# Lag blocks through device memory on POOL's queue, and a new order of convolution, norms, output halves and scan steps

## The chip, the cores and the metric

The program runs on 1 core of one Trainium2 chip. A core has TensorE (PE, matmuls), VectorE (DVE), ScalarE (ACT), GpSimd (POOL) and SyncE (SP), and 16 DMA engines that they share. The metric is the device time of one execution, in microseconds, as the median of several runs.

## The reference

One step of a hybrid backbone with one layer, on 128 context tokens and 512 latent tokens of width 1024. Both groups go through the same layer with their own modulation:

```python
def layer(x, cond, h0_f, h0_b, rows, p):
    sh1, sc1, g1, sh2, sc2, g2 = modulation(cond, p["w_mod"], p["b_mod"])
    h = rmsnorm(x, p["norm1_g"]) * (1 + sc1) + sh1
    y, h_f, h_b = token_mixer(h, h0_f, h0_b, rows, p)
    x = x + g1 * y
    h = rmsnorm(x, p["norm2_g"]) * (1 + sc2) + sh2
    x = x + g2 * peer(h, p["w_query"], p["sub_keys"], p["expert_u"], p["expert_v"])

def token_mixer(h, h0_f, h0_b, rows, p):
    u, cb, cc, ch = split(h @ p["w_in"])                  # 4 x 512
    y_ssm, h_f, h_b = ssm_mixer(u, h0_f, h0_b, p)         # 32 groups, 64 complex states, both directions,
                                                          # gelu, then a GLU with w_glu
    y_conv = cb * short_conv(cc * ch, p["conv_w"], p["conv_b"], rows)   # width 3
    y_ssm = rmsnorm(y_ssm, g[:D_SSM])
    y_conv = rmsnorm(y_conv per head of 64, g[D_SSM:])
    return concat(y_ssm, y_conv) @ p["w_out"], h_f, h_b
```

`peer` takes, for each token and each of 8 heads, the best 16 of 128 x 128 experts by product keys, and gathers two rows of 1024 floats for each: 640 tokens x 8 heads x 16 choices, 8 KB each. All is fp32.

## The kernel before, in words

Each engine has one program, written out by hand; semaphores join them. The scan over tokens is cut into chunks of 8 tokens: 16 of the context and 64 of the latents. The stage that the change touches runs from about 100 to 215 us, behind the modulation's first two thirds and the projection u, and ahead of the experts.

- *Modulation.* `w_mod` comes in 24 slabs of 1 MB (SP's `load_mod`, PE's `mod_slab`, 1 us each). From slab 8 on two buffers alternate, so slab n is loaded when slab n-2 is done.
- *Chunk sums.* For 16 groups g PE forms what each chunk adds to the states (`BPT` with `U`, into banks 4 and 5 in turn, `s_mm`). ACT copies each to the state array `HH`/`HHs` (`s_ev`), groups 8 to 15 of the backward direction in reversed order.
- *Lag blocks.* Within a chunk y is a sum over lags. PE forms the kernel of 15 lags (L645, `k_mm`), DVE puts it together in `Ksb` with the d_skip term (`lag_blocks`, `k_ev`), and PE selects from it by 128 small matmuls (L662) the Toeplitz blocks `M`, 128 x 128 for each of 32 groups, through banks that ACT copies out (L1217, `m_ev`).
- *Scan.* On DVE: 16 steps over the context's chunks (`scan_ctx`, then ACT's reversed copy `Hbc`), then 15 steps on the four latent segments at once, then the corrections of segments 2, 3 and 4 (`segment_products`, `segment_add`, `segment_store`), then `scan_lat`, whereupon ACT copies `Hb`.
- *Context.* PE: y (L697 to L702, needs `M`, `HH`, `Hbc`), `conv_ctx(0..2)` with 12 weight tiles of 512 KB that SP loads (`load_conv_ctx`; tile q is issued when tile q-4 is done), the turns of y, the GLU, `mod_turn(2)`, norms (`token_sums`, `spread_root`, `head_sums`, `spread_heads`), the output projection `out_ctx` (L788) with `w_o` (`woA`, `woB`), the second norm, the first query.
- *Latent y.* `y_lat(n, i)`, eight groups of 20 matmuls (L766 to L771), needs `M`, `HH` and `Hb`. Behind them PE selects the first experts (L864), DVE writes `gidx`, and POOL starts its gathers (L1935) with a ring of 8 and later 11 row buffers.
- *Experts.* 40 pairs of block and head, 16 gathers of 1 MB each; DVE forms the dot products (L1747), PE adds the weighted rows (L878). The latent half of the mixer is spread over the first 8 of them.

SP works its list in order. In before it issues `load_mod(18..23)`, waits for tile 2, then the two tiles of `w_glu`, tiles 6 and 7, `wqa`, tiles 8 and 9, and after slab 23 `woA` and tiles 10 and 11.

## Time and profile before

| | us |
|---|---|
| median of 3 runs | 1924.85 (1923.44 to 1925.14) |
| profiled execution, time | 1922.27 |
| its span, first to last instruction | 1920.1 |
| busy: PE, PE weight load | 1194.3, 475.8 |
| busy: DVE, ACT, POOL | 1382.6, 373.5, 725.1 |
| gathers L1935 | 640 |

The profile is one execution. A busy share is a mean over stages with different limits; here the first 215 us and the experts behind them differ. "L788" is line 788 of the kernel; an idle time is put down to what ended it. The clock is TensorE's granted one, as a share of full speed.

### The profile page before, as it was taken

The numbers are of one execution on the slowest core, as the hardware profiler recorded it, in microseconds if no ns is written. First come the engines' busy times: TensorE is split into PE (matmuls) and PEld (weight loads), VectorE is DVE, ScalarE is ACT, GpSimd is POOL, SyncE is SP. The second block draws the span as 40 slices with busy tenths as digits, with TensorE's granted clock in tenths as the row PEclk, the third lists the DMA queues.
The fourth block names the chain that finished last, engine by engine and source line by source line (L and its number), as shares of the span: only waits on it lengthen the run. The fifth ranks groups of instructions, "written<-read, shape, count | busy, mean of one in ns | idle before, by whom it ended". The sixth has DMA issues, their size and how long they took to land.

```text
span 1920.1 us, 21154 instructions
## 1 busy us (share of the span) xinstructions
PE 1194.3 (62%) x7716; PEld 475.8 (25%) x7716; DVE 1382.6 (72%) x3664; ACT 373.5 (19%) x845; POOL 725.1 (38%) x666
## 2 busy tenths in 40 slices
PE   6989898999777777775543343544343454444434
PEld 3569644444322322221110000111000011111001
DVE  8968567777766766669777776677777678766664
...
GB/s 372 328 209 199 257 395 414 378 416 420 390 421 399 419 422 421 420 389 422 420 422 423 421 421 421 421 421 421 422 422 421 421 421 418 422 420 421 418 420 182
DMA packets 120968, 753.16 MB, mean 392 GB/s; under 512 B 12240, under 2 KB 27856, under 8 KB 33568
## 3 DMA queue, kind: packets, MB, share of 16 engines
...
q1 hardware_dynamic: 28704, 80.69, 11.0%
...
## 4 chain that ended last, share of the span: by engine, by line
DMA 43%; PE 28%; DVE 23%; issue 2%; POOL 1%; ACT 1%; SPq 0%; DVEq 0%; POOLq 0%; ACTq 0%
DMA r<-table,gidx 31%; DVE r L1747 9%; DMA mix_r<-table,gidx 8%; PE bank L878 7%; PE bank L846 6%; PE bank L983 3%; DMA r<-w_mod 3%; DVE mix_r L1747 2%; PE bank L996 2%; PE bank L813 1%; POOL r L1935 1%; PE bank L962 1%; PE bank L855 1%; DVE i L1680 1%; PE bank L788 1%
## 5 line engine op out<-in xcount | busy, mean ns | idle before, releaser
L1935 POOL DMA_INDIRECT r<-table,gidx x542 | 607.7, 1121 | 865.3 <-PE bank L878 723.9
L1747 DVE CUSTOM_DVE_ANT_0 r<-r 128x1024 f32<-128x1024 f32 x542 | 658.1, 1220 | 246.5 <-DMA r<-table,gidx 246.0
L878 PE MATMUL bank<-r,cond 128*32 128x512 f32 x1432 | 327.2, 911 | 370.4 <-DVE cond L1759 295.2
L878 PE MATMUL bank<-r,wgt 128*32 128x512 f32 x736 | 166.8, 921 | 194.1 <-DVE wgt L1759 145.8
L1289 ACT ACTIVATE r<-r 128x2 f32<-128x2 f32 x320 | 65.1, 204 | 1013.1 <-DVE r L1747 1012.5
L878 PEld LDWEIGHTS bank<-r,cond 128*32 128x32 f32 x1432 | 37.1, 129 | 572.0 <-DVE cond L1759 437.2
L1935 POOL DMA_INDIRECT mix_r<-table,gidx x98 | 109.4, 1116 | 136.1 <-PE bank L878 117.0
L1747 DVE CUSTOM_DVE_ANT_0 mix_r<-mix_r,r 128x1024 f32<-128x1024 f32 x98 | 119.3, 1221 | 48.4 <-DMA mix_r<-table,gidx 48.2
L878 PE MATMUL bank<-mix_r,cond 128*32 128x512 f32 x264 | 91.1, 994 | 80.7 <-DVE cond L1759 63.4
L846 PE MATMUL bank<-hT_r,r 128*128 128x512 f32 x256 | 121.5, 630 | 0.9 <-ACT hT_r L1143 0.9
L878 PEld LDWEIGHTS bank<-r,wgt 128*32 128x32 f32 x736 | 18.9, 130 | 295.3 <-DVE wgt L1759 214.3
L1757 DVE SCALAR_TENSOR_TENSOR cond<-fold,r 128x32 f32<-128x32 f32 x168 | 34.8, 248 | 71.5 <-ACT r L1289 71.5
L846 PEld LDWEIGHTS bank<-hT_r,r 128*128 128x128 f32 x256 | 50.6, 203 | 75.8 <-issue 75.8
L1289 ACT ACT_TABLE_LOAD x51 | 65.4, 1283 | 0.9
L878 PE MATMUL bank<-mix_r,wgt 128*32 128x512 f32 x128 | 40.2, 930 | 38.2 <-DVE wgt L1759 35.6
L996 PE MATMUL bank<-mix_r,r 128*128 128x512 f32 x128 | 60.0, 611 | 0.0
L983 PE MATMUL bank<-hT_r,r 128*128 128x512 f32 x128 | 59.1, 604 | 0.0
L864 PEld LDWEIGHTS bank<-r,ident 128*32 128x32 f32 x1280 | 44.4, 140 | 43.6 <-DVE r L1719 36.8
L1747 DVE DVE_READ_ACCUMULATOR2_ANT r<- 128x1 f32 x640 | 52.6, 82 | 0.0
L1285 ACT ACT_TABLE_LOAD x40 | 51.3, 1283 | 0.7
L903 PE MATMUL bank<-mix_r,modrow 128*128 128x512 f32 x80 | 46.1, 712 | 3.2 <-ACT r L1304 1.9
L1757 DVE SCALAR_TENSOR_TENSOR wgt<-fold,r 128x32 f32<-128x32 f32 x88 | 18.3, 249 | 41.3 <-ACT r L1289 41.3
...
## 6 DMA issues: line engine op xcount, KB each, us to landing
r<-w_mod SPq DMA_DIRECT2D x24, 1024.0 KB, 9.7
r<-wq_heads SPq DMA_DIRECT2D x14, 1024.0 KB, 8.8
...
wq_heads<-w_query SPq DMA_DIRECT2D x8, 1024.0 KB, 12.1
r<-w_tiles SPq DMA_DIRECT2D x12, 512.0 KB, 7.8
x_r<-w_tiles SPq DMA_DIRECT2D x10, 512.0 KB, 6.0
...
r<-w_u SPq DMA_DIRECT2D x1, 2048.0 KB, 29.5
```

Of the source, the lines that this page charges most:

```text
L788: last = mm(bank[3 + m // 4][:, (m % 4) * P:(m % 4 + 1) * P], w[:, k, :], mixc[:, k, :], start=first and m in (0, 6) and k == ks[0], stop= ...
L846: last = mm(bank[2 + h][:, :], wqb[:, k, h * P:(h + 1) * P], hT[:, k, CTX:T], start=(k == 0), stop=(k == KD - 1))
L864: last = mm(bank[3][TG * s:TG * s + TG, 8 * tg:8 * tg + 8], ident[:, TG * tg:TG * tg + TG], gi[:, :, 4 * s:4 * s + 4], start=True, stop=True)
L878: last = mm(bank[ACC[b % 2][h]][to:to + TG, :], pair_weights(NPR * G + g)[:, e, :], rows[SLOT[G * TOPK + k]][:, D + h * 512:D + (h + 1) * ...
L903: last = mm(bank[at[h]][:, :], modrow[:, tg // 2, tg % 2 * P:(tg % 2 + 1) * P], h2tok[:, 512 * h:512 * h + 512], start=True, stop=True)
L983: last = mm(bank[(4, 5, 7)[r]][:, :], wtl[(tile + 2) % 3][:, k, :], hT[:, k, CTX:T], start=(k == 0), stop=(k == KD - 1))
L996: last = mm(bank[OUT_BANK[m % 3]][:, :], woA[:, m % 4, k, :], mixl[:, k, :], start=(k == 0), stop=(k == KD - 1))
L1285: A(e16, top, ACT.Exp, bias=small[:, 0:1], accum_out=small[:, 1:2]).then_inc(exp_done, 1)
L1289: A(gel[:, par, 2 * g:2 * g + 2], hid[:, par, 2 * g:2 * g + 2], ACT.Gelu_apprx_tanh).then_inc(gelu_done, 1)
L1747: V.tensor_tensor_reduce(row, row, h2r[tg], 1.0, 0.0, ALU.mult, ALU.add, hid[:, par, k:k + 1]).then_inc(dot_done, 1)
L1757: last = stt(pair_weights(n)[:, e, :], fold[:, :], gel[:, par, k:k + 1], gate[:, par, k:k + 1].broadcast_to([P, TG]), ALU.mult, ALU.mult)
L1935: G_.indirect_dma_start(rows[SLOT[j]], None, table, bass.IndirectOffsetOnAxis(gidx[:, e, k:k + 1], 0)).then_inc(row_in[SLOT[j]], 16)
```

## The change

- *Lag blocks.* PE's selecting matmuls and ACT's copies of them go. PE forms the lag kernel ahead of the chunk sums, DVE puts it together at once. POOL stores `Ksb` to `kfull` in device memory, waits for that and for chunk sums 0 to 7 (whose operand lies where `M` goes), and reads `M` back by eight loads, each for one position in the chunk, 16 partitions.
- *Chunk sums.* Groups 9, 11, 13 and 15 are copied by DVE (`s_back`).
- *PE's order.* Chunk sums, slabs 18 and 19, `conv_ctx(0)` and `(1)`, slabs 20 and 21, y, slabs 22 and 23, the turns, `conv_ctx(2)`, the GLU, `mod_turn(2)`, `head_sums`, `spread_heads`, then the convolution's half of the output projection, with the y norm within it, then the other half. All of latent y stands behind the first scores.
- *SP's order.* Each buffer's tile comes when its predecessor is done, in the new order; `wqa` behind slab 23, `woA` and tiles 10 and 11 still behind the wait for slab 23.
- *DVE.* A step's two cross products become one with its operand reversed, in `segment_products` too. The long steps are cut up (`advance_rest`), with the convolution, the norms and the halves of `mixc` between them. The residual lies ahead of segment 3, the second norm between segments 3 and 4.
- *ACT.* The order of its operations follows; `Hb` is copied behind the first scores.

The diff, cut to its core (the full order is in the list above):

```diff
                 load_conv_ctx(q)
-            for n in range(18, 24):
-                load_mod(n)
-            sp.wait_ge(zc_mm, 2)
+            load_mod(18)
+            load_mod(19)
+            for q in range(6, 8):
+                load_conv_ctx(q)
             for j in range(2):
                 sp.dma_start(wt[:, j, :, :], w_tiles[NCONV + j]).then_inc(wtg_in, 16)
-            for q in range(6, 8):
-                load_conv_ctx(q)
-            sp.wait_ge(m_mm, 2)
-            sp.dma_start(wqa, w_query[:, :, 0:DQ]).then_inc(ld_first, 16)
+            load_mod(20)
+            load_mod(21)
             for q in range(8, 10):
                 load_conv_ctx(q)
+            load_mod(22)
+            load_mod(23)
+            sp.wait_ge(lag_dma, 16)
+            sp.dma_start(wqa, w_query[:, :, 0:DQ]).then_inc(ld_first, 16)
             sp.wait_ge(mod_mm, 24)
             sp.dma_start(woA, w_o[:, 0:4, :, :]).then_inc(ld_wo, 16)
             for q in range(10, 12):
...
-                if g >= 2:
-                    pe.wait_ge(s_ev, g - 1)
+            def chunk_sums(g):
+                if g >= 10 and g % 2:
+                    pe.wait_ge(s_back, (g - 9) // 2)
+                elif g >= 2:
+                    pe.wait_ge(s_ev, min(g - 1, 4 + g // 2))
                 for j in range(2):
...
                             last = mm(bank[4 + g % 2][64 * a:64 * a + 64, (2 * j + r) * NCH:(2 * j + r + 1) * NCH],
                                       BPT[:, q, r, 64 * a:64 * a + 64], U[:, 2 * (q % NPAIR) + a, :], start=True, stop=True)
                 last.then_inc(s_mm, 1)
-                if g == 7:
-                    mod_slab(17)
             pe.wait_ge(bd_ready, 1)
...
             mod_slab(18)
             mod_slab(19)
-            pe.wait_ge(k_ev, 1)
-            pe.wait_ge(s_ev, 16)
-            for a in range(2):
...
-                        row = slice(TG * j, TG * j + TG)
-                        col32 = slice(s // 2 * TG, s // 2 * TG + TG)
-                        last = mm(bank[MBANK[a][j]][col32, :], esel[row, a, s % 2, :], Ksb[row, :, lag0:lag0 + P],
-                                  start=(s % 2 == 0), stop=(s % 2 == 1))
-                last.then_inc(m_mm, 1)
-                mod_slab(20 + a)
-            mod_slab(22)
             def conv_ctx(r):
-                pe.wait_ge(m_ev, (1, 2, 5)[r])
                 for i in range(4):
                     q = 4 * r + i
                     pe.wait_ge(wtc_in[WTC[q]], WTC[:q + 1].count(WTC[q]) * 16)
                     for k in range(KD):
                         last = mm(bank[r][:, i * P:(i + 1) * P], wtc[WTC[q]][:, k, :], hT[:, k, 0:CTX], start=(k == 0), stop=(k == KD - 1))
                     last.then_inc(zc_mm, 1)
-                    if r == 2 and i == 0:
-                        pe.wait_ge(chx_ev, 1)
...
-                        spread_root(0)
-            pe.wait_ge(m_ev, 8)
+            conv_ctx(0)
+            conv_ctx(1)
+            mod_slab(20)
+            mod_slab(21)
+            pe.wait_ge(lag_dma, 16 * (Q + 1))
+            pe.wait_ge(s_ev, 12)
+            pe.wait_ge(s_back, 4)
+            pe.wait_ge(k_ev, 1)
             pe.wait_ge(hbc_ready, 1)
             for i in range(4):
                 for term in range(5):
...
-            conv_ctx(0)
+            mod_slab(22)
...
-                pe.wait_ge(inv_ready, 2)
+                pe.wait_ge(inv_ready, 1)
                 for m in range(KS):
                     for h in range(2):
...
                 last.then_inc(inv_mm, 1)
-            mod_slab(23)
-            conv_ctx(1)
+            conv_ctx(2)
             pe.wait_ge(wtg_in, 32)
             pe.wait_ge(gtc_ev, 2)
...
-            conv_ctx(2)
+            head_sums()
+            spread_heads()
...
                 for m in (0, 1, 2, 3, 6, 7, 4, 5) if first else range(KD):
-                    if first and m == 2:
-                        head_sums()
                     if first and m == 6:
-                        spread_heads()
+                        pe.wait_ge(sqc_ready, 2)
+                        token_sums(256, sqx[0], True, True)
+                    if first and m == 4:
+                        spread_root(0)
                     if m == 4:
                         pe.wait_ge(ld_wob, 16)
...
             pe.wait_ge(ld_wo, 32)
-            out_ctx(True, range(KS), 1)
-            out_ctx(False, range(KS, KD), 2)
+            out_ctx(True, range(KS, KD), 1)
+            out_ctx(False, range(KS), 2)
             pe.wait_ge(sqc_ready, 3)
             token_sums(257, sqx[0], True, False)
-            pe.wait_ge(hb_ready, 1)
-            pe.wait_ge(mod_free, 6)
-            y_lat(0, 0)
             pe.wait_ge(sqc_ready, 4)
             token_sums(257, sqx[1], False, True)
-            y_lat(0, 1, range(1))
             spread_root(1)
-            y_lat(0, 1, range(1, 5))
             def query(u, halves=range(2)):
...
-            for i in range(4):
-                y_lat(1, i)
+            pe.wait_ge(hb_ready, 1)
+            pe.wait_ge(mod_free, 6)
+            for n in range(2):
+                for i in range(4):
+                    y_lat(n, i)
             spread_experts(0)
             turn_rows(0)
...
-            for g in range(16):
+            for g in (*range(8), *range(8, 16, 2)):
...
+            act.wait_ge(zc_mm, 4)
+            A(ccx.rearrange("p k t -> p (k t)"), bank[0][:, :], ACT.Copy).then_inc(ccx_ev, 1)
             act.wait_ge(scan_ctx, 1)
             A(Hbc[:, 0:NCC, :, :], HH[:, NCC - 1::-1, :, 1, :], ACT.Copy).then_inc(hbc_ready, 1)
             for a in range(2):
                 act.wait_ge(yc_mm, a + 1)
                 A(Yc.rearrange("p t (i a c) -> p t i a c", i=4, a=2)[:, :, :, a, :],
                   bank[4 + a][:, :].rearrange("p (i t c) -> p t i c", i=4, t=Q), ACT.Gelu_apprx_tanh).then_inc(yc_gelu, 1)
-            act.wait_ge(zc_mm, 4)
-            A(ccx.rearrange("p k t -> p (k t)"), bank[0][:, :], ACT.Copy).then_inc(ccx_ev, 1)
...
+            A(sqx[1], mixc[:, KS:KD, :].rearrange("p k t -> p (k t)"), ACT.Square).then_inc(sqc_ready, 1)
+            act.wait_ge(sqc_used, 1)
+            A(rt8, bank[1][:, 264:272], ACT.Sqrt, scale=1.0 / (DC // 8), bias=eps_c[:, 0:1]).then_inc(rms_c, 1)
             act.wait_ge(zgc_mm, 1)
             for m in range(KS):
                 A(mixc[:, m, :], bank[5][:, m * P:(m + 1) * P], ACT.Sigmoid, bias=col(COL_BGLU + m)).then_inc(sgc_ev, 1)
             mod_take(2)
             act.wait_ge(gluc_ev, 1)
             A(sqx[0], mixc[:, 0:KS, :].rearrange("p k t -> p (k t)"), ACT.Square).then_inc(sqc_ready, 1)
-            act.wait_ge(sqc_used, 1)
+            act.wait_ge(sqc_used, 2)
             A(rt1[0], bank[1][:, 256:257], ACT.Sqrt, scale=1.0 / DS, bias=eps_c[:, 0:1]).then_inc(rms_c, 1)
-            act.wait_ge(cvx_ev, 1)
-            A(sqx[1], mixc[:, KS:KD, :].rearrange("p k t -> p (k t)"), ACT.Square).then_inc(sqc_ready, 1)
...
+            act.wait_ge(scan_lat, 1)
+            A(Hb, HH[:, NCH - 1:NCC - 1:-1, :, 1, :], ACT.Copy).then_inc(hb_ready, 1)
             exps(0)
             for n in range(2):
...
-                link(tt(ta, prev, re, ALU.mult),
-                     tt(tb[:, :, 0, :], prev[:, :, 1, :], im[:, :, 0, :], ALU.mult),
-                     tt(tb[:, :, 1, :], prev[:, :, 0, :], im[:, :, 1, :], ALU.mult))
+                link(tt(ta, prev, re, ALU.mult), tt(tb, prev[:, :, ::-1, :], im, ALU.mult))
                 link(tt(ta, ta, cur, ALU.add))
                 return tt(cur, ta, tb, ALU.add)
...
+            for g in range(9, 16, 2):
+                pr = g % 8 * 2
+                dve.wait_ge(s_mm, g + 1)
+                for r in range(2):
+                    src = bank[4 + g % 2][:, 0:4 * NCH].rearrange("p (q r c) -> p c r q", q=2, r=2)[:, :, r, :]
+                    V.tensor_copy(HH[:, NCC:0:-1, r, 1, pr:pr + 2], src[:, 0:NCC, :])
+                    last = V.tensor_copy(HH[:, NCH - 1:NCC:-1, r, 1, pr:pr + 2], src[:, NCC + 1:NCH, :])
+                last.then_inc(s_back, 1)
+            dve.wait_ge(s_back, 4)
+            dve.wait_ge(s_ev, 12)
             link(V.tensor_copy(fin[:, :, :], HHs[:, NCC, :, :]))
             link(V.tensor_copy(HHs[:, NCC, :, :], ssmv[:, 3:5, :]), V.memset(HHs[:, 0, :, :], 0.0))
             for i in range(1, NCC):
                 link(advance(HHs[:, i - 1:i, :, :], HHs[:, i:i + 1, :, :], step_a, step_b, spread(AR, 1), spread(AI, 1)))
-                if i == 3:
-                    lag_blocks()
             advance(HHs[:, NCC - 1:NCC, :, :], fin[:, :, :].rearrange("p (a r) x -> p a r x", a=1), step_a, step_b,
                     spread(AR, 1), spread(AI, 1)).then_inc(scan_ctx, 1)
             rest = slice(1, NJ)
-            for i in range(1, SEG):
-                link(advance(seg[:, rest, i - 1, :, :], seg[:, rest, i, :, :], many_a, many_b, spread(AR, NJ - 1), spread(AI, NJ - 1)))
...
+            def advance_rest(lo, hi):
+                for i in range(lo, hi):
+                    link(advance(seg[:, rest, i - 1, :, :], seg[:, rest, i, :, :], many_a, many_b, spread(AR, NJ - 1), spread(AI, NJ - 1)))
             def segment_products(j):
                 last = HHs[:, j * SEG - 1:j * SEG, :, :].broadcast_to([P, SEG, 2, NQ])
                 link(tt(seg_a, last, PR.rearrange("p i (a x) -> p i a x", a=1).broadcast_to([P, SEG, 2, NQ]), ALU.mult),
...
             def segment_add(j):
...
             cw = [[col(COL_CW + tap * KS + i) for i in range(KS)] for tap in range(3)]
+            ccx1 = ccx.rearrange("p k t -> p (k t)")
+            advance_rest(1, 7)
             dve.wait_ge(ccx_ev, 1)
             dve.wait_ge(zc_mm, 8)
...
+            advance_rest(7, 10)
+            dve.wait_ge(zc_mm, 12)
+            tt(mixc[:, KS:KD, :].rearrange("p k t -> p (k t)"), cvx.rearrange("p k t -> p (k t)"), bank[2][:, :], ALU.mult).then_inc(cvx_ev, 1)
+            advance_rest(10, 12)
+            dve.wait_ge(rms_c, 1)
+            V.reciprocal(inv8, rt8).then_inc(inv_ready, 1)
+            advance_rest(12, 13)
+            dve.wait_ge(inv_mm, 1)
+            dve.wait_ge(cvx_ev, 1)
+            for m in range(KS):
+                last = stt(mixc[:, KS + m, :], mixc[:, KS + m, :], col(COL_OG + KS + m), bank[0][:, m * P:(m + 1) * P], ALU.mult, ALU.mult)
+            last.then_inc(mixc_ready, 1)
             dve.wait_ge(sgc_ev, KS)
             tt(mixc[:, 0:KS, :], mixc[:, 0:KS, :], gTc, ALU.mult).then_inc(gluc_ev, 1)
-            link(*[stt(cvx[:, i, 0:CTX - 1], ccx[:, i, 1:CTX], cw[2][i], cvx[:, i, 0:CTX - 1], ALU.mult, ALU.add) for i in range(KS)])
-            segment_products(2)
-            dve.wait_ge(rms_c, 1)
+            advance_rest(13, 15)
+            dve.wait_ge(rms_c, 2)
             V.reciprocal(inv1[0], rt1[0]).then_inc(inv_ready, 1)
-            segment_add(2)
-            dve.wait_ge(inv_mm, 1)
+            advance_rest(15, 16)
+            dve.wait_ge(inv_mm, 2)
             dve.wait_ge(gluc_ev, 1)
             for m in range(KS):
                 last = stt(mixc[:, m, :], mixc[:, m, :], col(COL_OG + m), bank[1][:, 0:P], ALU.mult, ALU.mult)
             last.then_inc(mixc_ready, 1)
+            dve.wait_ge(yc_gelu, 2)
+            dve.wait_ge(gtc_mm, 2)
+            segment_products(2)
+            segment_add(2)
             segment_store(2)
-            dve.wait_ge(zc_mm, 12)
-            tt(mixc[:, KS:KD, :].rearrange("p k t -> p (k t)"), cvx.rearrange("p k t -> p (k t)"), bank[2][:, :], ALU.mult).then_inc(cvx_ev, 1)
-            segment_products(3)
-            dve.wait_ge(rms_c, 2)
-            V.reciprocal(inv8, rt8).then_inc(inv_ready, 1)
-            segment_add(3)
-            segment_store(3)
-            dve.wait_ge(inv_mm, 2)
-            dve.wait_ge(cvx_ev, 1)
-            for m in range(KS):
-                last = stt(mixc[:, KS + m, :], mixc[:, KS + m, :], col(COL_OG + KS + m), bank[0][:, m * P:(m + 1) * P], ALU.mult, ALU.mult)
-            last.then_inc(mixc_ready, 1)
-            segment_products(4)
-            segment_add(4)
-            segment_store(4)
-            V.tensor_copy(small[:, 2:3], eps_c[:, :]).then_inc(scan_lat, 1)
             dve.wait_ge(ld_xc, 16)
-            for h in range(2):
+            def residual_ctx(h):
                 dve.wait_ge(zoc_mm, h + 1)
                 for j in range(4):
                     m = 4 * h + j
                     last = stt(xtc[:, m, :], bank[3 + h][:, j * P:(j + 1) * P], modT[:, 2 * KD + m, 0:1], xtc[:, m, :], ALU.mult, ALU.add)
                 last.then_inc(x1c_ready, 1)
+            residual_ctx(0)
+            residual_ctx(1)
+            segment_products(3)
             dve.wait_ge(rms_c, 3)
             V.reciprocal(inv1[1], rt1[1]).then_inc(inv_ready, 1)
             gains(4, COL_N2, 6)
+            segment_add(3)
+            segment_store(3)
             dve.wait_ge(inv_mm, 3)
             dve.wait_ge(x1c_ready, 2)
...
+            segment_products(4)
+            segment_add(4)
+            segment_store(4)
+            V.tensor_copy(small[:, 2:3], eps_c[:, :]).then_inc(scan_lat, 1)
             NT = 23
...
+            pool.wait_ge(k_ev, 1)
+            G_.dma_start(kfull.rearrange("(m p) x -> p m x", p=P), Ksb).then_inc(lag_dma, 16)
+            pool.wait_ge(s_mm, 8)
+            pool.wait_ge(lag_dma, 16)
+            lags = kfull.rearrange("(g i) x -> i g x", i=GC)
+            for i in range(Q):
+                G_.dma_start(M[GC * i:GC * i + GC, :, :], lags[:, :, (Q - 1 - i) * GC:(Q - 1 - i) * GC + P]).then_inc(lag_dma, 16)
             pool.wait_ge(mod_tr, 6)
             G_.tensor_copy(modrow.rearrange("p h (g s i) -> p (h g) s i", g=2, s=4),
```

## Rows read from the trace of the kernel before

**Rows 1.** The page, part 2: GB/s moved in 40 slices of 48 us.

```profile
GB/s 372 328 209 199 257 395 414 378 416 420 390 421 399 419 422 421 420 389 422 420 422 423 421 421 421 421 421 421 422 422 421 421 421 418 422 420 421 418 420 182
```

**Rows 2.** Timeline of POOL: start us, us, engine, line, operation [idle before].

```profile
215.58 1.12 POOL L1935 DMA_INDIRECT r<-table,gidx  x1 [48.58 <-DVE gidx L1731]
217.00 0.94 POOL L1935 DMA_INDIRECT r<-table,gidx  x1 [0.30 <-issue]
```

**Rows 3.** Chain of waits, 95 to 235 us: start us, us, what.

```profile
181.90 10.91 PE bank L788 x96
```

**Rows 4.** Timeline of PE, 95 to 215 us; x counts matmul records.

```profile
104.19 5.54 PE L631 MATMUL bank<-r 128*64 128x80 f32 x128
...
120.09 2.06 PE L645 MATMUL bank<-r 128*32 128x128 f32 x68 [1.60 <-issue]
...
124.17 3.93 PE L662 MATMUL bank<-mix_r,wgt 32*32 32x512 f32 x64 [0.19 <-DVE mix_r L1560]
...
129.35 4.79 PE L662 MATMUL bank<-mix_r,wgt 32*32 32x512 f32 x64
...
144.87 3.84 PE L675 MATMUL bank<-hT_r,r 128*128 128x128 f32 x32
...
198.79 3.81 PE L826 MATMUL bank<-hT_r,mix_r 128*128 128x128 f32 x32 [0.33 <-ACT hT_r L1143]
...
205.43 0.66 PE L766 MATMUL bank<-r 128*64 128x128 f32 x8
...
213.99 0.88 PE L864 MATMUL bank<-r,ident 128*32 128x8 f32 x32
```

**Rows 5.** Timeline of DVE, 95 to 262 us.

```profile
136.69 0.42 DVE L1571 TENSOR_TENSOR r<-r,AR 128x256 f32<-128x256 f32 x1
...
138.47 0.43 DVE L1571 TENSOR_TENSOR r<-r,AR 128x256 f32<-128x256 f32 x1
...
182.05 1.12 DVE L1645 SCALAR_TENSOR_TENSOR mix_r<-mix_r,colv,bank 128x128 f32<-128x128 f32 x4
183.09 1.22 DVE L1598 TENSOR_TENSOR r<-r 128x1024 f32<-128x1024 f32 x1
...
188.14 0.15 DVE L1650 COPY small<-eps_c 128x1 f32<-128x1 f32 x1
...
197.37 0.69 DVE L1664 TENSOR_TENSOR hT_r<-x_r,bank 128x512 f32<-128x512 f32 x1 [0.51 <-PE bank L731]
...
198.69 1.12 DVE L1668 TENSOR_SCALAR hT_r<-hT_r,gs,modT 128x128 f32<-128x128 f32 x4
```

**Rows 6.** Timeline of ACT, 95 to 215 us.

```profile
188.33 1.91 ACT L1244 ACTIVATE r<-r 128x2048 f32<-128x2048 f32 x1 [9.03 <-DVE small L1650]
```

**Rows 7.** Windows: stretch, its us, busy per engine, clock, DMA share, GB/s.

```profile
104.26:192.65 88.39, 82.82 (x1350) 70.01 (x1351) 65.60 (x212) 26.78 (x80) 0.61 (x1) 1.00 0.59 216
...
112.00:116.00 4.00, 3.80 (x82) 3.24 (x82) 0.00 (x0) 3.19 (x22) 0.00 (x0) 1.00 1.03 430
...
234.00:236.00 2.00, 2.00 (x11) 1.39 (x8) 1.97 (x7) 0.23 (x1) 1.05 (x1) 0.50 1.03 430
```

**Rows 8.** DMA issues of the whole run: KB each, us from issue to landing.

```profile
r<-w_o SPq DMA_DIRECT2D x1, 2048.0 KB, 11.0
x_r<-w_o SPq DMA_DIRECT2D x2, 1024.0 KB, 4.9
...
x_r<-xT SPq DMA_DIRECT2D x1, 512.0 KB, 4.4
```

**Rows 9.** The same, issued from 158 to 163 us alone.

```profile
x_r<-w_tiles SPq DMA_DIRECT2D x3, 512.0 KB, 10.3
```

**Rows 10.** Timeline of PE, 228 to 244 us.

```profile
229.28 1.04 PE L928 MATMUL bank<-ident,mix_r 128*128 128x128 f32 x8
233.31 1.38 PE L878 MATMUL bank<-r,wgt 128*32 128x512 f32 x8 [2.99 <-DVE wgt L1757]
234.62 1.97 PE L928 MATMUL bank<-ident,mix_r 128*128 128x128 f32 x8
```

44 lines of the change are left out of this document (15 added, 29 removed).

## Prediction

> **What bounds the kernel now.** I read the page first. In slices of 48 us its GB/s row stands near 420 from slice 6 to the end [rows 1]: the expert stage is one stream of gathers. The change touches nothing in it. It moves work that ends before the first gather, which POOL issues at 215.58 us [rows 2]. So the question is how much earlier or later that stream starts. I take every microsecond there one for one, since the bytes and matmuls behind it stay.
>
> The chain of waits between 95 and 235 us says what sets that start. It passes through the scan on DVE, then the convolution of the context on PE, the output projection L788 (181.9 to 192.8 without a break [rows 3]) and the latent y matmuls L766 to L771, behind which the experts' selection L864 stands at 213.99 [rows 4]. The timelines of PE, DVE and ACT give the lengths of the steps [rows 4 to 6]. By the windows view PE is busy for 82.82 of the 88.39 us from 104.26 to 192.65, so idle for 5.57, and DVE for 65.60 [rows 7]. PE is the bound of this stage. The reader should see two things: work taken off PE counts in full here, and so does a new hole on PE.
>
> I call z the moment at which the output projection of the context is done, 192.65 in before. From z to the selection at 213.99 it takes 21.3 us.
>
> **The change part by part, up to z.**
>
> *Removed:* the 128 selecting matmuls L662, in two halves 3.93 + 4.79 = 8.7 us of PE [rows 4]; ACT's eight copies of them lay in its idle time. The 5.6 us of holes in before go too; of these 1.60 ("issue", ahead of the second half of L645 [rows 4]) has no releaser in the trace, so it may come back elsewhere: between 0 and 1.6, I take 0.8.
>
> *Added, lag blocks by POOL:* one store of the 480 KB of Ksb to device memory, a wait for it, then eight loads of 256 KB, each in 512 pieces of 512 bytes. Before has no such store or load on this queue. The nearest row is a gather of 128 rows: 0.94 us, and 0.30 between two [rows 2]. Bound from below: a load costs POOL the same, 1.24. From above: it grows with the pieces, 4 x 0.94 + 0.3 = 4.1. For the data there is one row with such pieces, the 512 KB load of xT that landed in 4.4 us [rows 8]; four times its data, with its latency once, is 8 to 10 us. The lag kernel is ready near 110.4 (K matmuls L645 3.9 us from 104.4, scaled from 68 of 128 records in 2.06 [rows 4], then some 2 us on DVE), the store lands at 115 to 119, the eight loads are issued 10 to 33 us later and land 2.5 us after that: at 128 in the best case, 154 in the worst, 140 in the middle (2.6 us each). PE asks for them at 142 (below). No row decides between the ends, so I take the middle, which costs 0, and keep +12 as the upper bound.
>
> The Trainium skill ("SBUF — State Buffer", its box on the trap "DVE blocks DMA") speaks against this part: while DVE runs a fp32 tensor_copy between SBUF tiles in a two-port mode, POOL can't write the descriptors of its own queue. No row here shows it. The same page says that tensor_tensor has no two-port mode, and the scan consists of these, so by the rule the sum stays as it is.
>
> *K matmuls first, then the chunk sums, four groups of them copied by DVE:* an order, not work. Groups keep PE's own pace of 5.54 / 8 = 0.69 us [rows 4] to the end, -0.4. The K matmuls wait 0.15 for the d_skip column. The scan starts some 4 us later than in before, but the lag kernel no longer interrupts it and each step merges two products (1.78 to about 1.72 for a long step [rows 5], as much for a short one): it ends near 136.7, as before, and PE isn't at y yet.
>
> *Two convolution groups and slabs 20, 21 ahead of y:* PE would reach y at 139.1: from 104.4 on, 3.9 of K, 12.1 of chunk sums and slab 17, 2.0 for two slabs, eight tiles at 1.85 (two took 3.84 with their tail [rows 4]) 14.8, two slabs 2.0. But SP issues tile 6 only when tile 2 is done (128.0), and behind it tile 7, two GLU tiles, slabs 20 and 21: 4.2 MB. At 430 GB/s, the rate at 112 to 116 [rows 7], that is 9.8 us, plus 2.4 of latency (a 1 MB load of w_o landed in 4.9, 2.4 of it data [rows 8]): slab 21 lands at 140.2, is done on PE at 141.2, and about 1 us later with POOL's loads in between. PE waits 3.3 us; bounds 2 and 5.
>
> *w_o and tiles 10, 11:* SP holds the 2 MB of woA until slab 23 is done and queues tiles 10 and 11 behind it, in the same order as before. After, slab 23 comes right ahead of the turns (1.0) and tiles 8 and 9 (3.7). 2.6 MB need 6.1 + 2.4 = 8.5 us. That makes a hole of 3.8 us; the GLU matmuls, which could fill it, stand behind tile 11.
>
> *Norms and output halves:* between head_sums and spread_heads come Sqrt and reciprocal, 0.6 us. Then DVE does a scan step (1.78) and four products (1.12 [rows 5]) while PE has 1.0 of spreading: 1.9. Together 2.5.
>
> So z moves by -8.7 - 5.6 + 0.8 + 0.15 - 0.4 + 3.3 + 3.8 + 2.5 = -4.1 us, to 188.5. Without any hole it would be 104.26 + 82.82 - 8.7 = 178.4.
>
> **From z on.** In before, two of the eight latent y groups fill PE's idle time during the norm, and the scan is done at 188.3, Hb at 190.2 [rows 5, 6]. After, DVE still has segments 3 and 4. Its order is residual 1.2, segment 3 (183.09 to 188.14: 5.05), norm (197.37 to 199.8: 2.4), segment 4 5.05, marker 0.15 [rows 5], then ACT's Hb copy 1.91 [rows 6]. Less 0.15 for the merged products, with 0.3 for the small instructions and handing over: 15.9 us from z. The first query (3.81 [rows 4]) fits beside segment 4. Only then come all eight y groups, at (213.99 - 205.43) / 5 = 1.71 each [rows 4], 13.7, and the selection: 29.6 us instead of 21.3, +8.2. DVE's top-k starts before y and is the shorter. Without the clock the sum is +4.1 us.
>
> **The clock.** After PE had idled for 2.99 us [rows 10] its granted clock was 0.50 at 234 to 236 [rows 7], 1.2 GHz of 2.4; eight turns took 1.97 instead of 1.04 [rows 10]. After has three holes of that length that before has not: ahead of tile 10 (3.8), in the norm after z (about 4, with spread_root alone in it) and before Hb (2 to 3). A fall like that doubles some 3 us of matmuls. Behind the first, tiles 10, 11 and the GLU matmuls stand on the path: 2.5. The second slows the first query, half hidden by segment 4, the third slows y: together 1.5. Bounds 0 and 9, I take 4.0. The Trainium skill ("TensorE: Matmul & The Clock Gate", Part 1) says that an idle array is gated to 1.2 GHz and that activity releases it; by that rule a hole costs twice, and the trace agrees.
>
> Sum: +4.1 + 4.0 = +8.1 us. The profiled execution has a span of 1920.1 and a time of 1922.27, 2.6 under the runs' median of 1924.85; added to the median: 1933.0.
>
> **Rivals.**
> *Holes on PE, as above* (slower): 1929 to 1941. For it: the orders of SP, PE and DVE, step by step. Chance 0.49.
> *Lag blocks late* (slower): POOL's loads cost near 4.1 us each and y waits until 154, 12 us on top: 1945. It decides from 2.9 us a load on. For and against it: nothing in the trace. Chance 0.17.
> *No difference:* the clock stays up and the tiles land a little sooner: +0 to +3.8, about 1927. For it: the holes of 1.6 and 0.2 in before cost no clock. Chance 0.20.
> *PE stays fed, faster:* one mechanism, SP's loads. If slabs 20, 21 and tiles 10, 11 overtake the big loads, and the norm is covered, z is 178.4 and 29.6 later y ends at 208.0: -6.0 us, 1918.9. It decides at z under 180.5. Against it: three tiles issued around woA in before landed in 10.3 us, when woA itself took 11.0 [rows 8, 9]. Chance 0.14.
>
> **The numbers.** 0.2% is 3.8 us, about what a measurement of this kernel tells from no change. Slower 0.49 + 0.17 = 0.66, within 0.20, faster 0.14. The range goes from 1922, which leaves out "faster" and little else, to 1946, the late lag blocks at their bound.
>
> **What would show it.** In the profile after: L662 gone; a wait of PE for w_mod near 140 us; one for w_tiles ahead of tile 10; PE waiting for Hb after the first scores; eight y groups in one block; the first gather near 224; a clock of 0.50 between 150 and 210. The prediction is wrong if POOL's loads land after 145 (then worse), if PE shows no wait at tile 10, if the clock stays at 1.00 (then +4), or if the start moves and the end doesn't.

## The result: slower by 1.7%, four times the forecast loss

After: 1955.75 us (median of 4 runs, 1954.65 to 1957.41). Before, beside it on the same chip: 1924.14 us. The ratio is 1.0168 [1.0150, 1.0186]. The forecast was 1933.0 (1922 to 1946). The direction was right; 1955.75 lies above the range, and the loss of 31.6 us compares with a forecast of 8.1. The profiled execution took 1954.65 us with a span of 1952.9, 32.8 more than before.

The page's part 2, with GB/s in slices of 48.8 us, answers [rows 1]: all that differs lies in the first five slices.

```profile
GB/s 375 323 211 233 44 401 395 392 403 416 406 407 410 379 422 423 421 415 407 421 422 422 422 422 422 421 421 421 422 421 421 421 422 416 420 422 417 419 417 186
```

The timeline of POOL answers [rows 2]. The eight loads cost POOL 5.04 us together, and the first gather is issued 29.7 us later than in before:

```profile
109.75 0.99 POOL L1927 DMA_DIRECT2D kfull<-mix_r  x1 [7.42 <-DVE mix_r L1545]
118.81 5.04 POOL L1932 DMA_DIRECT2D r<-kfull  x8 [8.07 <-PE bank L636]
...
245.30 1.04 POOL L1946 DMA_INDIRECT r<-table,gidx  x1 [56.30 <-DVE gidx L1734]
```

From the first gather to the end it is 1707.6 us, in before 1704.5; across the kernels profiled here this stretch varies between 1704 and 1711. So the rest of the text looks at the time before the gather.

The timeline of TensorE answers [rows 4]:

```profile
143.10 6.28 PE L666 MATMUL bank<-hT_r,x_r 128*128 128x128 f32 x32 [8.95 <-DMA x_r<-w_tiles]
149.42 1.07 PE L531 MATMUL bank<-r,cond 128*32 128x256 f32 x16
151.91 1.07 PE L531 MATMUL bank<-r,cond 128*32 128x256 f32 x16 [1.42 <-DMA r<-w_mod]
152.80 0.62 PE L688 MATMUL bank<-r 128*32 128x128 f32 x16
...
158.30 0.31 PE L693 MATMUL bank<-r 64*16 64x128 f32 x4 [2.65 <-issue]
...
163.68 0.42 PE L688 MATMUL bank<-r 128*32 128x128 f32 x8 [1.02 <-issue]
...
177.23 6.29 PE L666 MATMUL bank<-hT_r,x_r 128*128 128x128 f32 x32 [5.58 <-DMA x_r<-w_tiles]
...
193.30 6.75 PE L781 MATMUL bank<-mix_r,r 128*128 128x128 f32 x32 [1.36 <-DVE mix_r L1624]
...
208.15 3.74 PE L781 MATMUL bank<-mix_r,x_r 128*128 128x128 f32 x32
...
219.51 5.64 PE L814 MATMUL bank<-hT_r,mix_r 128*128 128x128 f32 x32 [3.45 <-ACT hT_r L1132]
...
228.60 0.66 PE L758 MATMUL bank<-r 128*64 128x128 f32 x8 [2.27 <-ACT r L1358]
...
243.72 0.88 PE L852 MATMUL bank<-r,ident 128*32 128x8 f32 x32
```

Three things stand out. TensorE waits 8.95, 5.58 and 3.45 us, and the 32 matmuls behind each of these take 6.28, 6.29 and 5.64 us where they need 3.74 to 3.81 at full clock; the first 32 of the output projection, behind a row of small waits, take 6.75. The granted clock, the third number from the end, says that all four ran at 0.50:

```profile
143.00:148.00 5.00, 4.89 (x23) 4.90 (x24) 4.15 (x11) 0.00 (x0) 0.00 (x0) 0.50 1.03 420
177.50:182.00 4.50, 4.50 (x22) 4.50 (x23) 0.00 (x0) 0.00 (x0) 0.00 (x0) 0.50 0.28 117
193.50:199.00 5.50, 5.50 (x27) 5.50 (x28) 3.39 (x9) 1.92 (x2) 0.00 (x0) 0.50 0.02 3
220.00:223.00 3.00, 3.00 (x16) 3.00 (x15) 2.97 (x6) 0.52 (x2) 0.00 (x0) 0.50 0.00 1
```

The context outputs (L688 to L693) take 152.80 to 165.12, 12.3 us; in before the same matmuls took 7.3. Two idle times in them, of 2.65 and 1.02 us, are marked "issue": no releaser is known for them. And z, the end of the context's output projection, is 211.72 instead of 192.65, the selection 243.72 instead of 213.99: 32.0 us from z on, where before took 21.3.

The windows view (stretch, its length, busy time of PE, PEld, DVE, ACT, POOL, clock, DMA share, GB/s) answers [rows 7]:

```profile
118.00:125.00 7.00, 6.55 (x119) 5.21 (x115) 4.57 (x26) 1.26 (x8) 5.04 (x8) 1.00 0.91 160
125.00:130.00 5.00, 5.00 (x47) 5.00 (x47) 4.42 (x22) 0.00 (x0) 0.00 (x0) 1.00 1.06 104
130.00:135.00 5.00, 4.15 (x38) 3.96 (x36) 4.45 (x23) 0.60 (x1) 0.00 (x0) 1.00 1.05 105
135.00:140.00 5.00, 0.00 (x0) 0.00 (x0) 4.62 (x17) 1.91 (x2) 0.00 (x0) 0.80 1.03 107
140.00:160.00 20.00, 12.79 (x232) 10.30 (x236) 15.88 (x43) 0.00 (x0) 0.00 (x0) 0.76 1.01 391
```

Here is the surprise. For fifteen microseconds all 16 DMA engines are busy and move a quarter of what they moved in [rows 7]: 104 to 107 GB/s, against 430. The queue view of 125 to 130 (packets, MB, share of 16 engines) shows who has them:

```profile
q0 software_dynamic: 159, 0.52, 105.7%
```

Only POOL's queue is in that list. SP issues tile 6 at 128.8, and the trace has no packet of SP's queue between 120.2 and 138.5; the last packets of the lag blocks end at 141.8.

### The profile page after: what moved, and what is told of

Same layout as the page of the kernel before. It is cut to its first block, busy times and chain, and to the rows that moved or that the text cites. A ratio compares the mean times of both kernels' runs of the same rounds, so it can differ in the third digit from the quotient of the medians.

```text
span 1952.9 us, 20863 instructions
## 1 busy us (share of the span) xinstructions
PE 1201.9 (62%) x7588; PEld 482.0 (25%) x7588; DVE 1381.9 (71%) x3646; ACT 367.8 (19%) x822; POOL 732.9 (38%) x675
## 4 chain that ended last, share of the span: by engine, by line
DMA 40%; PE 33%; DVE 21%; issue 3%; ACT 2%; POOL 1%; SPq 0%; DVEq 0%; POOLq 0%; ACTq 0%
DMA r<-table,gidx 24%; DMA mix_r<-table,gidx 12%; DVE r L1750 8%; PE bank L866 8%; PE bank L834 6%; DMA r<-w_mod 4%; PE bank L971 3%; PE bank L984 3%; DVE mix_r L1750 2%; PE bank L801 1%; PE bank L891 1%; POOL r L1946 1%; PE bank L781 1%; PE bank L843 1%; DVE i L1683 1%
## 5 line engine op out<-in xcount | busy, mean ns | idle before, releaser
L891 PE MATMUL bank<-mix_r,modrow 128*128 128x512 f32 x80 | 51.0, 778 | 3.2 <-ACT r L1287 1.9
L852 PE MATMUL bank<-r,ident 128*32 128x8 f32 x1280 | 46.8, 195 | 1.4 <-DVE r L1722 1.4
## 6 DMA issues: line engine op xcount, KB each, us to landing
r<-w_mod SPq DMA_DIRECT2D x24, 1024.0 KB, 11.5
wq_heads<-w_query SPq DMA_DIRECT2D x8, 1024.0 KB, 11.5
x_r<-w_tiles SPq DMA_DIRECT2D x10, 512.0 KB, 10.1
```

What stands on the lines that cost most here:

```text
L852: last = mm(bank[3][TG * s:TG * s + TG, 8 * tg:8 * tg + 8], ident[:, TG * tg:TG * tg + TG], gi[:, :, 4 * s:4 * s + 4], start=True, stop=True)
L891: last = mm(bank[at[h]][:, :], modrow[:, tg // 2, tg % 2 * P:(tg % 2 + 1) * P], h2tok[:, 512 * h:512 * h + 512], start=True, stop=True)
```

## The experiments

The first set takes the lag loads apart. Kernels of one set shared their runs of before (1924.57 us here).

**No loads** (lag blocks are not loaded, and TensorE waits for the store alone; the outputs are formed with what lies in M):

```diff
-            for i in range(Q):
-                G_.dma_start(M[GC * i:GC * i + GC, :, :], lags[...]).then_inc(lag_dma, 16)
```

> The changed kernel without POOL's eight loads of the lag blocks (the store stays), so the lag term of y is formed with whatever lies in M. In the changed kernel the DMA engines are busy from 118 to 141 us at about 105 GB/s, and no packet of SP's tiles moves in that time. Theory A (the loads themselves hold all engines, and the tiles wait behind them): the 8.95 us wait at tile 6 goes or falls under 2, the clock stays up at tile 6, and the first gather moves from 245.3 to 228 to 234; time 1936 to 1943. Theory B (SP's order of loads is the cause, the lag blocks only beside it): the wait at tile 6 stays above 5 us, time above 1950.

Measured: 1945.02 us, ratio 1.0107 [1.0090, 1.0124]. The wait at tile 6 is gone; tiles 2 to 7 run as one row:

```profile
127.16 10.88 PE L666 MATMUL bank<-hT_r,x_r 128*128 128x128 f32 x96
141.00 1.26 PE L531 MATMUL bank<-r,cond 128*32 128x256 f32 x16 [2.96 <-DMA r<-w_mod]
143.50 1.94 PE L531 MATMUL bank<-r,cond 128*32 128x256 f32 x16 [1.25 <-DMA r<-w_mod]
155.10 0.43 PE L688 MATMUL bank<-r 128*32 128x128 f32 x8 [3.06 <-issue]
```

So the loads cost 10.7 of the 31.6 us; without them the time lies inside the forecast's range. The wait at slabs 20 and 21 is now 4.2 us; the forecast had 3.3.

**Spread** (the same bytes and pieces on the same queue, but every load goes to all 128 partitions; the blocks hold other values):

```diff
+            rows_of = kfull.rearrange("(m p) x -> p m x", p=P)
-                G_.dma_start(M[GC * i:GC * i + GC, :, :], lags[...])
+                G_.dma_start(M[:, 4 * i:4 * i + 4, :], rows_of[:, :, GC * i:GC * i + P])
```

> The changed kernel with the same eight loads on POOL's queue, same bytes and same 512 pieces of 512 bytes each, but each load writes 128 partitions (4 pieces in each) instead of 16 partitions (32 pieces in each). It reads the pieces from other places of the stored lag kernel, so M holds other values. Theory A1 (writing to 16 neighbouring partitions is what holds the rate at 105 GB/s): the loads are through in 6 to 9 us at 250 GB/s or more, and the time falls to within 4 us of that without loads. Theory A2 (512-byte pieces on POOL's queue are slow whatever they write): the rate stays near 105 GB/s for some 20 us, and the time within 3 us of 1955.8.

Measured: 1946.26 us, 1.0115 [1.0098, 1.0132], as without any loads. POOL's queue in this kernel at 120 to 125, 125 to 127 and 127 to 129:

```profile
q0 software_dynamic: 426, 1.43, 98.0%
q0 software_dynamic: 175, 0.58, 99.1%
q0 software_dynamic: 33, 0.07, 11.1%
```

That is 1.43 MB in 5 us, 286 GB/s by this queue, where the changed kernel's queue moves 0.52 MB. The 2 MB are in by about 127 instead of 142. The source rows and the size of the pieces are the same; what differs is where they land, and with it the order in which the rows are read. So the slow form is the one in which a load's destination is 16 neighbouring partitions.

**SP's queue** (the narrow loads issued by SP behind slab 19):

```diff
+                sp.dma_start(M[GC * i:GC * i + GC, :, :], lags[...]).then_inc(lag_in, 16)
```

> The changed kernel with the eight loads on SP's queue, behind slab 19 and ahead of tile 6, same 16-partition shape. A1 (partitions): rate again near 105 GB/s, some 20 us, time 1950 to 1960. A2 (POOL's queue is slow with small pieces): over 200 GB/s, time 1938 to 1945.

Measured: 1953.45 us, 1.0146 [1.0129, 1.0163]; 99 GB/s at 125 to 130, a wait of 8.16 us at tile 6. POOL's queue is not to blame: the way of issuing hardly changes the rate (99 for 104) or the wait (8.16 for 8.95).

**Tiles first** (tiles 10 and 11 ahead of the wait for slab 23 and woA):

```diff
+            for q in range(10, 12):
+                load_conv_ctx(q)
             sp.wait_ge(mod_mm, 24)
             sp.dma_start(woA, w_o[:, 0:4, :, :]).then_inc(ld_wo, 16)
-            for q in range(10, 12):
-                load_conv_ctx(q)
```

> The changed kernel with tiles 10 and 11 issued ahead of the wait for slab 23, so ahead of woA. If the 5.6 us wait at tile 10 and the low clock behind it come from the 2 MB of woA in front: the wait goes, tiles 10 and 11 take 3.7 us instead of 6.3, time falls by 6 to 9 us, to 1947 to 1950. If SP's order doesn't matter there: same time as the changed kernel, 1955.8.

Measured: 1947.78 us, 1.0124 [1.0107, 1.0141], 8.0 us less than the changed kernel, as expected. The hole at tile 10 was priced at 3.8 and measures 5.58; with the slow tiles behind it, it is worth 8.0.

The second set (before: 1923.49 us) asks where the other 20 us are.

**Quiet outputs** (no loads, and SP holds everything behind slab 21 until the context outputs are done; a single execution):

```diff
             load_mod(21)
+            sp.wait_ge(yc_mm, 2)
```

> The changed kernel without the eight loads, as in the first run (the lag term is formed with what lies in M), and SP holds tiles 8 and 9, slabs 22 and 23 and wqa until y of the context is done, so the DMA engines are idle while PE runs y. Without that hold y took 12.1 us (145.2 to 157.3) instead of the 7.3 of before, with an idle stretch of 3.06 that nothing in the trace released, at a DMA share of 1.0. Theory I (PE's instructions arrive through the same DMA engines and are late behind SP's loads): y takes 7 to 8.5 us, no idle stretch over 0.5 without releaser in it. Theory C (the low clock alone makes y long): y still takes 11 us or more and the idle stretch stays. The whole is slower or equal, since slabs 22 and 23 come late.

Measured: 1949.3 us. The figure to read is in the stage itself: the context outputs run from 143.84 to 151.4, 7.5 us instead of 12.3, and one short hole is left. The third row is all that the DMA engines carried at 143 to 152 besides one packet of the other instruction queue:

```profile
143.00:152.00 9.00, 7.85 (x336) 5.54 (x328) 8.55 (x26) 0.59 (x2) 0.00 (x0) 0.97 0.03 6
...
149.91 0.42 PE L689 MATMUL bank<-r 128*32 128x128 f32 x8 [0.58 <-issue]
...
q8 instruction: 3, 0.05, 2.5%
```

With the DMA engines silent (6 GB/s) the "issue" holes of up to 3.6 us shrink to 0.58. Without the loads but without the hold, the one other difference, the context outputs took 12.1 us (145.2 to 157.3) with a hole of 3.06; a part of these 12.1 was low clock. In the changed kernel the stretch 152 to 166 has a DMA share of 0.71 and 268 GB/s, in before 137 to 145 has 0.30 and 119. The kernel as a whole is slower than without the loads (1945.02), because slabs 22 and 23 now come late (a wait of 8.91).

The trace lists two queues "instruction" among those of the DMA engines. Queue q8 brings 60 packets of 16 KB in before, for 15432 instructions of TensorE (matmuls and weight loads), about 257 each. And it settles what ends the holes. In the changed kernel packets of q8 end at 156.89 and 162.22, and the matmuls go on at 158.30 and 163.68, 1.41 and 1.46 us later. In the quiet form it is 148.45 and 149.91 (1.46), without the loads 153.66 and 155.10 (1.44), in before 141.44 and 142.86 (1.42). All 43 "issue" holes that TensorE's timelines show between 100 and 216 us, in the fourteen traces of this case, end 1.2 to 1.6 us after such a packet has. So these are waits for instructions, and the instructions come through the engines that carry SP's tiles. The packets of the long holes do not take longer than the others (all take 0.88 to 1.24 us); they begin later. The same packet begins at 155.74 in the changed kernel, 2.9 us behind the first of these matmuls, and at 143.74 in the quiet form, 0.1 us ahead of it. That full engines delay their beginning is what the quiet form speaks for; which transfer stood ahead of them is not shown. The Trainium skill ("Runtime: NRT & Kernel Launch", section "Instruction fetch mechanics") says that each engine refills its small instruction memory in blocks through a DMA queue of its own, and that the cost is mostly hidden. The first half agrees with the trace (q8, packets of 16 KB); the second did not hold here, with holes of 2.65 and 1.02 us.

**Selection by TensorE again** (after's order, but the lag blocks made by L670 and ScalarE's copies as in before, nothing on POOL):

```diff
+            for a in range(2):
+                for s in range(Q):
+                    ...
+                        last = mm(bank[MBANK[a][j]][col32, :], esel[row, a, s % 2, :], Ksb[row, :, lag0:lag0 + P], ...)
-            pe.wait_ge(lag_dma, 16 * (Q + 1))
+            pe.wait_ge(m_ev, 8)
```

> The changed kernel with the lag blocks made on PE again (128 selecting matmuls behind slab 19, ACT's eight copies) and no store and no loads on POOL's queue; all else in the new order. If the way through device memory is a net loss: PE gets 8.7 us of work, loses the 8.95 us wait at tile 6 and its low clock, and the time is 1946 to 1951. If the selecting matmuls cost in full and the waits stay: 1960 or more.

Measured: 1955.46 us, 1.0163 [1.0148, 1.0179]. That is 4.5 us above the range expected, and it says something plain: the new order, with nothing on POOL, loses as much as the whole change. The selection takes 122.84 to 134.4 here, 11.5 us, since it now stands behind the sums, waits 1.67 for ScalarE and runs its second half in 5.95:

```profile
122.84 3.93 PE L670 MATMUL bank<-mix_r,wgt 32*32 32x512 f32 x68
128.43 5.95 PE L670 MATMUL bank<-mix_r,wgt 32*32 32x512 f32 x60 [1.67 <-ACT r L1221]
```

Tiles 6 and 7 no longer wait, but the slabs (2.81 and 1.42), the "issue" holes (0.32 and 3.32) and tile 10 (5.72) do. The way through device memory saves the selection and loses 10.7 to its narrow loads: a draw.

**Merged products alone** (before, with DVE's two cross products of a scan step in one instruction):

```diff
-                     tt(tb[:, :, 0, :], prev[:, :, 1, :], im[:, :, 0, :], ALU.mult),
-                     tt(tb[:, :, 1, :], prev[:, :, 0, :], im[:, :, 1, :], ALU.mult))
+                     tt(tb, prev[:, :, ::-1, :], im, ALU.mult))
```

> The kernel before with one part of the change alone: the two cross products of a scan step, and those of a segment, as one instruction with its operand reversed. A step's period falls by 0.06 us; the scan is on the path from 122 to 168 us (14 short and 15 long steps), with hand-overs to PE. If the path follows it: first gather 1 to 2 us earlier, time 1922.5 to 1924. If PE is the bound there: no difference.

Measured: 1922.64 us against 1923.49, 0.9992 [0.9982, 1.0001]. The first gather came 2.5 us earlier, the time shows no difference beyond its uncertainty. (The profiled execution, 1925.57 us, was also the slowest of the 11.) It is the one part of the change that was tried alone on before, and it does no harm.

**TensorE kept at work** (matmuls whose result nobody reads, in four holes):

```diff
+                    if q == 6:
+                        pe.wait_ge(s_back, 4)
+                        keep_busy(16)
+                    if q == 10:
+                        keep_busy(9)
```

> The changed kernel with extra matmuls on PE, 128x512, whose result nobody reads, where it stood idle: 16 ahead of tile 6, 9 ahead of tile 10, 6 behind spread_root(1), 4 ahead of the wait for Hb. They are sized to end before the waits do. If the low clock costs what its rows show (tiles 6 and 7 6.3 instead of 3.7 us, tiles 10 and 11 the same, the first output half 6.8 for 3.7, the first query 5.6 for 3.8): clock at 1.00 from 142 to 150, 177 to 184 and 219 to 226, and 6 to 10 us less, 1946 to 1950. If the clock falls for another reason or doesn't matter: 1955 to 1958.

Measured: 1953.41 us, 1.0151 [1.0136, 1.0167]. Too many: the fillers before tile 6 ran 13.9 us and pushed it from 143.1 to 149.8. But the matmuls behind each ran at full clock. Hence a second size, 8, 4, 3 and 2 (before: 1924.5, as for the next two kernels):

> The changed kernel with TensorE kept at work in its holes by matmuls whose result nobody reads, half as many as in the run that overran (8 of 128x512 before convolution tile 6, 4 before tile 10, 3 after the second root is spread, 2 before the wait for the latent states); the output is the same. At 0.87 us each they fill 7.0 of the 8.95 us hole, 3.5 of 5.58, 2.6 of 3.45 and 1.7 of 2.27, so none should push its successor back. Clock theory: the holes cost what they last and besides that a stretch at half clock behind each (tiles 6,7 6.28 for 3.73 us, tiles 10,11 6.29 for 3.74, out half 6.75 for 3.74, query 5.64 for 3.8, first selections 8.76 for 7.1); with the fillers these run at full clock and the time falls by 6 to 9 us, to 1947 to 1950. Rival: the low clock is already hidden behind transfers and DVE, so the successors are released by something else: above 1953.

Measured: 1948.65 us, 1.0122 [1.0107, 1.0137], 7.1 us less than the changed kernel, as expected. The rows behind the fillers (L663):

```profile
136.55 7.03 PE L663 MATMUL bank<-hT_r,ones 128*128 128x512 f32 x16
...
144.75 3.84 PE L676 MATMUL bank<-hT_r,x_r 128*128 128x128 f32 x32 [1.17 <-DMA x_r<-w_tiles]
...
174.78 3.60 PE L663 MATMUL bank<-hT_r,ones 128*128 128x512 f32 x8
179.25 3.84 PE L676 MATMUL bank<-hT_r,x_r 128*128 128x128 f32 x32 [0.87 <-DMA x_r<-w_tiles]
...
214.33 4.31 PE L663 MATMUL bank<-hT_r,ones 128*128 128x512 f32 x6
218.48 3.73 PE L826 MATMUL bank<-hT_r,mix_r 128*128 128x128 f32 x32
```

Tiles 6, 7 and tiles 10, 11 take 3.84 us for 6.28 and 6.29, the first query 3.73 for 5.64. At tile 6 that gains little, since slab 20 is then waited for (2.49 us). The first gather comes 4.2 us earlier (241.15), though this execution entered the stage 2.3 us later than the changed kernel's (lag kernel matmuls at 106.14 for 103.87); the modrow matmuls behind it take 7.10 for 8.76. So filling four holes gives back 4 to 7 us. It is not the whole price: with the fillers the clock is still 0.50 at 190.2 to 197.0, where the first output half takes 6.04, and 0.51 at 152.6 to 159.5. In the changed kernel the rows at low clock add up to some 12 us over full clock ahead of the first gather (2.5 at tile 6, 1.0 in the context outputs, 2.6 at tile 10, 3.0 at the output half, 1.8 at the query, 1.3 in the latent outputs), part of it hidden behind waits. The forecast had 4.0, with a bound of 9.

**Tail back** (DVE runs the long scan steps and segments 2 and 3 in its idle time ahead of tile 12, ScalarE copies Hb early, two groups of the latent outputs stand again ahead of the first query):

```diff
-            advance_rest(7, 10)
+            advance_rest(7, 16)
+            dve.wait_ge(yc_gelu, 2)
+            dve.wait_ge(gtc_mm, 2)
+            for j in (2, 3):
+                segment_products(j)
+                segment_add(j)
+                segment_store(j)
             dve.wait_ge(zc_mm, 12)
```

> The changed kernel with the tail's order set back: DVE runs the last scan steps and segments 2 and 3 in its 25 us without work ahead of the wait for convolution tile 12, segment 4 among the norms, ScalarE makes the copy Hb ahead of the query, TensorE runs the first two groups of the latent outputs between the token sums, as the kernel before did. Everything ahead of tile 12 stays as it is. Tail theory (the 10.7 us by which the stretch from the end of the output halves to the selection grew comes from the order of DVE and of the latent outputs): that stretch is 22 to 24 us instead of 32.0, the rest unchanged, 1946 to 1949. Rival (DVE's segments ahead of the tile push the context part back, or the latent outputs just move into a stretch in which TensorE is bound anyway): 1952 or more.

Measured: 1942.39 us, 1.0096 [1.0081, 1.0110], 13.4 us less than the changed kernel; 7 to 10 were expected. z is at 212.26 (211.72 in the changed kernel), the first query waits 0.33 us instead of 3.45 and runs in 3.81, and the selection comes at 233.59:

```profile
218.40 3.81 PE L819 MATMUL bank<-hT_r,mix_r 128*128 128x128 f32 x32 [0.33 <-ACT hT_r L1136]
...
233.59 0.88 PE L857 MATMUL bank<-r,ident 128*32 128x8 f32 x32
```

The stretch from z is 21.3 us, exactly that of before. Of the 13.4 us, 10.1 lie ahead of the first gather (235.18 for 245.30).

**Combined** (spread loads, other values in M; slabs 20, 21 ahead of tiles 6, 7; tiles 8 to 11 ahead of slabs 22, 23; tail back):

> The changed kernel with four repairs at once, output the same: lag blocks loaded into all 128 partitions in strided order (their content is permuted, so this part is for time only), SP's queue with slabs 20, 21 ahead of tiles 6, 7 and tiles 8 to 11 ahead of slabs 22, 23 and the output weights, and the tail's order set back. Additive theory: 1955.8 less 9.5 (spread loads) less 8.0 (tiles 10, 11 first) less 8 (tail) less 1.4 (slab wait) gives 1929, range 1926 to 1933, so nearly all of the loss is these; about 5 us above the kernel before would be left, for the instruction holes in the chunk outputs and for the clock behind what waits are left. Rival: the repairs overlap (each gives back the same wait of TensorE for data), 1936 or more.

Measured: 1937.43 us, 1.0069 [1.0057, 1.0081], within the rival's range, but not by its mechanism. The trace doesn't show repairs that give back the same wait for data; it shows a new one. The convolution is done at 166.5, earlier than in the kernel with the tail back alone, and DVE, then about to begin segments 2 and 3, takes up the result of tile 12 only at 177.1:

```profile
178.64 1.84 PE L713 MATMUL bank<-headones,mix_r 128*128 128x2 f32 x8 [7.11 <-ACT mix_r L1217]
```

**Combined, second form** (segment 2 alone ahead of tile 12, segments 3 and 4 among the norms; lag blocks to their own places in 32 loads that take turns):

```diff
+            for w in range(4):
+                for i in range(Q):
+                    g = slice(8 * w, 8 * w + 8)
+                    G_.dma_start(M[GC * i:GC * i + GC, g, :], lags[:, g, ...]).then_inc(lag_dma, 16)
```

> The changed kernel with the order repairs of the combined run, a complete computation this time: the lag blocks go to their own places, each 16-partition load cut into four that take turns, so that neighbours in the queue write to different sixteenths of the partitions (32 loads); SP's queue with slabs 20, 21 ahead of tiles 6, 7 and tiles 8 to 11 ahead of slabs 22, 23; and DVE runs only segment 2 ahead of convolution tile 12, segments 3 and 4 among the norms. Destination theory in its strong form (only what is next to each other in the queue matters): the loads run well above 105 GB/s, as in the strided form, TensorE's wait for DVE ahead of the head sums (7.1 us in the combined run) is gone, and the time is 1929 to 1934, still above the kernel before. Rival (all engines work on one load at a time, so turns don't help): 99 to 115 GB/s between 120 and 140, convolution tile 6 late by some 8 us again and slabs 20, 21 too, 1938 to 1945.

Measured: 1930.04 us (10 runs), 1.0036 [1.0024, 1.0049] against before (1922.97). The first gather is issued at 220.25. TensorE's wait for DVE is gone. The loads take POOL 16.73 us (0.52 each), and the engines now move more in all:

```profile
125.00:130.00 5.00, 5.00 (x47) 5.00 (x46) 4.45 (x23) 0.00 (x0) 5.00 (x11) 1.00 1.04 317
130.00:135.00 5.00, 3.90 (x35) 3.71 (x34) 4.44 (x23) 0.60 (x1) 5.00 (x10) 1.00 1.00 230
```

The lag blocks themselves are not faster. By queue they moved 0.24, 0.62 and 0.52 MB at 125 to 130, 130 to 135 and 135 to 140, so 48, 124 and 104 GB/s, and they end at 145.8, 4 us later than in the changed kernel; the context outputs even wait 1.19 us for them. What changed is the share of the engines that they take: 14.9, 58.4 and 36.8% instead of all. Between 119 and 137 SP's queue moved 2.93 MB beside 1.42 MB of lag blocks; in the changed kernel it moved 0.08 MB beside 1.86. Taking turns and cutting the loads up came together here, so which of the two frees the engines is not shown. This version keeps the change's lag blocks, convolution and norms, without its tail, and gives back 25.7 of the 31.6 us, but it doesn't beat before. No version tried here does beyond the measurement's uncertainty.

## Why the forecast was right or wrong, step by step

- **Lag blocks by POOL: the step that failed.** POOL's price was bounded by 1.24 to 4.1 us a load and measures 0.63, below both bounds; the rival "lag blocks late" through POOL's issue did not happen. The data was priced at "8 to 10 us" by one xT row with 512-byte pieces whose destination is 128 partitions. It took some 21 us for 2.1 MB at about 105 GB/s, from 120.2 to 141.8. The lag blocks themselves were not late (y, the context outputs, began at 152.8); what came late was tile 6, which the forecast let SP load at 430 GB/s "about 1 us later with POOL's loads in between". That term of 1, within the 3.3 for PE's wait at the slabs (bound 5), measures 10.7 by the kernel without loads and 9.5 by the one with spread loads. So the wait named in the forecast stood in the wrong place, at slabs 20 and 21 instead of at tile 6, and was too small. The Trainium skill ("SBUF — State Buffer", Door 1) had the price: it lists 104 GB/s measured for a transfer to partitions 0 to 15 and 328 for all 128. The trace agrees, with 104 to 107. It was cited for another rule and not for this one.
- **The context outputs, taken over unchanged.** 7.3 us in before, 12.3 in after. The forecast moved SP's loads beside this stage and did not ask what else uses the DMA engines. 5.0 us, of which 3.7 are "issue" holes, waits for instruction packets, and the rest matmuls at low clock behind the first of them. The quiet form (7.5 us) ties them to the load on the engines.
- **The hole at tile 10.** Right in place and cause, 5.58 for 3.8; worth 8.0 with its clock.
- **The clock.** Right in kind and too small. The forecast counted three falls, ahead of tile 10, in the norm behind z and ahead of Hb; all three came (0.50 at 177.5 to 182, at 220 to 223, and again in the latent outputs at 231 to 233). It missed those behind tile 6, in the context outputs and at the first output half. Filling four holes gave back 4 to 7 us and left low stretches, so the term of 4.0 was at most right and more likely short.
- **Slabs 20, 21.** 3.3 forecast, 1.42 measured behind the longer wait, 4.2 without the lag loads.
- **From z on.** 29.6 plus 1.5 of clock forecast, 32.0 measured, and 10.7 us above before. With the order set back it is 21.3. This was the best part of the forecast, in mechanism and size: segments 3 and 4 do stand behind z, and all eight groups of outputs behind them.
- **The scan's end** was forecast for 136.7 and came at 137.3.
- **The gain.** The 8.7 us of L662 did go. The kernel with TensorE's selection and the new order is as fast as the change (1955.46), so in the new order that gain went to the narrow loads. By the forecast's own terms that kernel would have been some 8.7 us slower than 1933; it is 22 us slower, so the order too was priced too low.
- **Sum.** z was forecast at 188.5 and came at 211.72, 23.2 us later. Ahead of y 10.4 (y began at 152.80, where 142.4 was forecast), y 5.0, up to tile 10 1.6 (12.1 from the end of y, forecast 2.0 + 1.0 + 3.7 + 3.8); the remaining 6.2 come between there and z, most of it matmuls at low clock (6.29 and 6.75 for 3.74 each). From z on 2.4 more came. Of these 25.6 us the forecast had 4.0 in its clock term.
- **The signs.** L662 was gone, PE waited at tile 10 and for Hb (2.27 us), the eight y groups stood in one block, the clock fell to 0.50 between 150 and 210, and POOL's loads had landed before 145. The wait for w_mod came at 151.9 instead of near 140, and the first gather at 245.30 instead of near 224; no sign asked about a wait at tile 6 or within the context outputs.
- **The chances.** "Slower" held 0.66 and came; that was no luck, since the tail (13.4 us by its experiment) and the hole at tile 10 (8.0) were foreseen as losses. The range ended at 1946 because each rival stood alone in it: holes on PE, or a late transfer. What came was both together, and a stage slowed by its neighbour that no rival had.

Still open: why the repaired form stays 7 us above before. It has a wait of 3.91 us at tile 6, one of 1.19 for the lag blocks and "issue" holes of 0.86 and 3.31; that these are the 7 us was not tried. Nor was the 2.5 us earlier gather of the merged products followed to the end of the span.
